# Layer 1's convolution norm: GpSimd adds the blocks and their squares ahead of one product of ones each, a gate tile later

## The chip, the cores and the metric

One core of a Trainium2 chip runs the whole kernel. The metric is the device time of one launch in microseconds (us), the median over several launches. The engines are named TensorE (PE; its weight loads are shown apart, PEld), VectorE (DVE), ScalarE (ACT), GpSimd (POOL) and SyncE (SP), which issues the weight transfers.

## The reference

A backbone of two layers. Each layer projects its normed input once, feeds three parallel branches (attention, a Conformer convolution, a short gated convolution), merges them by sigmoid gates, and adds a SwiGLU feed-forward. Layer 0 works on 256 latent and 256 context tokens, layer 1's branches on the 256 latent tokens alone. The change is in the layer norm of the convolution branch, over its 256 channels:

```python
def layer_norm(x, g, b):
    mu = jnp.mean(xf, axis=-1, keepdims=True)
    var = jnp.mean(jnp.square(xf - mu), axis=-1, keepdims=True)
    y = (xf - mu) * lax.rsqrt(var + EPS)
    return (y * g.astype(jnp.float32) + b.astype(jnp.float32)).astype(x.dtype)

def conformer_conv(glu_in, dw, dw_b, ln_g, ln_b, w_out):
    a, g = jnp.split(glu_in, 2, axis=-1)
    u = depthwise_conv(a * jax.nn.sigmoid(g), dw) + dw_b
    u = jax.nn.silu(layer_norm(u, ln_g, ln_b))
    return u @ w_out

def merge_branches(gate_in, y_att, y_conv, y_sc, w_o):
    g_att, g_conv, g_sc = jnp.split(jax.nn.sigmoid(gate_in), N_BRANCH, axis=-1)
    return (g_att * y_att + g_conv * y_conv + g_sc * y_sc) @ w_o
```

## The kernel before

Channels lie on the 128 partitions, tokens along the free axis, so the 256 convolution channels are two blocks, `ACC[:, 0]` and `ACC[:, 1]`. Each engine runs its own program in a fixed, hand-written order, and the engines meet at semaphores.

**Products.** Every float32 weight is split into a high and a low part so that TensorE can multiply with three fast products (lines 2000 to 2002). A weight piece arrives in one of four slots `Wraw` by a transfer that SyncE issues as soon as the slot's last residual is out (`load`, line 448, waits on `lo_done`). ScalarE converts it to `Whi` (line 399, `split_hi`, first waiting until the slot's last tile is done), VectorE makes the residual `Wlo` (line 410, `split_lo`), and TensorE's `chunk()` waits for that. Both helpers are called `look` and run three pieces ahead of TensorE (`AHEAD = 3`). GpSimd's `look` only counts.

**The branch stage** of a layer is eight groups. In a group TensorE makes two gate tiles (24 products each, from wide pieces 128x1024) and two output tiles (6 products each, from narrow pieces 128x256): groups 0 to 3 the outputs of the short convolution, groups 4 to 7 those of the Conformer convolution. A product has 512 columns in layer 0 and 256 in layer 1. ScalarE's `group` copies each gate tile out by a tanh into `TG` (line 783) once the output of the group before that used the same half of `TG` is drained. VectorE's `group` joins tanh and output (lines 1743 and 1748), which frees the output's bank. Tiles go round four PSUM banks.

**The norm** is woven into groups 2 and 3. VectorE finishes `ACC` (line 1780, semaphore `conv_a`). TensorE multiplies it with a matrix of ones, which gives the mean over channels in a bank; VectorE centres `ACC` (`centred`, line 1760), ScalarE squares it into `SQ` (`mean_squares`, line 1063, `conv_sq`), TensorE multiplies the squares with ones, ScalarE takes the root (`root`, line 801), and VectorE's `scaled` takes the reciprocal (line 1360) and applies it, gain and bias (lines 1768 and 1771). Then ScalarE's tanh, VectorE's product (line 1788, `conv_s`) and ScalarE's and VectorE's high and low part (lines 830 and 1367) make the operand `CO0` that the output tiles of group 4 wait for (`op_lo`). Root and tanh lie in different tables of ScalarE, which shows as ACT_TABLE_LOAD.

In layer 0 GpSimd adds the two blocks of `ACC`, and later the two of `SQ`, into `SUM`, and TensorE does one product of ones each (`of_sum`, line 2604), the mean after gate tile 1 of group 2 and the squares after gate tile 0 of group 3. In layer 1 TensorE does two products for each (`over_channels`, line 2564), the mean after gate tile 0 of group 2 and the squares between groups 2 and 3. In layer 1 alone eight transposes ahead of the mean (`gate_row`, line 2317) make a row that ScalarE copies into `LINES`.

Of the kernel before, what the change touches and what calls it, by code (L numbers as in the profile page):

```python
# [12 lines left out]
CH = 256  # L13
# [30 lines left out]
BEFORE_LAYER = 3  # L44
ROOT_AFTER = 12
LAST_BRANCH, LAST_FF = 39, 67
MEAN_AFTER = [1, 0]
PARTS = 4
PART = DT // PARTS

# [115 lines left out]
def build(nc, x, c, ctx_in, c_ctx, w_mod, b_mod, ln1_g, w_in, q_a_norm_g, w_q_b, kv_a_norm_g,  # L166
# [6 lines left out]
    with stack:  # L173
# [463 lines left out]
        def _(pool):  # L637
# [55 lines left out]
            for l in range(DEPTH):  # L693
                TQ = NS[l] * SEQ
                nxt = ahead(projection_kinds(l), HEAD_KINDS)

                def step_in():
                    look(next(nxt))

                clear_sum(stat_root(l, 0))  # L700
                if l == 0:
                    next(nxt)
                for _ in range(5 if l else 4):
                    step_in()
                at.square.n += 2
                for _ in range(2):
                    add_square(TQ)
                    step_in()
                at.square.next()
                for _ in range(9):  # L710
                    step_in()
                pool.wait_ge(tap_head, l + 1)
                pool.wait_ge(root_done, stat_root(l, 2))
                for w in range(TAPS_BEFORE, TAPS):
                    pool.wait_ge(pool_step, step.now())
                    v = mark(pool.tensor_scalar(by_stream(SUM[:, :], l), U[:, 1, 0:NS[l], w:w + SEQ],  # L716
                                                PAR[:, l, CDW + 2 * w + 1:CDW + 2 * w + 2], None, ALU.mult))
                    pool.wait_ge(pool_step, v)
                    ins = pool.tensor_tensor(by_stream(ACC[:, 1, :], l), by_stream(ACC[:, 1, :], l),  # L719
                                             by_stream(SUM[:, :], l), ALU.add)  # L720
                    if w < TAPS - 1:
                        mark(ins)
                    else:
                        ins.then_inc(tap_tail, 1)
                pool.wait_ge(tap_tail, l + 1)
                for kind in ["plain", "keys", queries_kind(1)]:
                    look(kind)
                with at.loop(pool, PAIRS - 2, chunks=4):
                    for kind in pair_looks(0):
                        look(kind)  # L730
                for p in range(PAIRS - 2, PAIRS):
                    for kind in pair_looks(p):
                        look(kind)
                for kind in ahead(["plain"] * 4, branch_kinds(l)):
                    look(kind)
                with at.loop(pool, 3, chunks=8):
                    for kind in ahead(branch_kinds(l), branch_kinds(l)):
                        look(kind)
                for kind in ahead(branch_kinds(l), ["plain"] * AHEAD):
                    look(kind)  # L740
                if l == 0:
                    pool.wait_ge(root_done, stat_root(l, 2))
                    pool.wait_ge(conv_a, 1)
                    pool.tensor_tensor(SUM[:, :], ACC[:, 0, :], ACC[:, 1, :], ALU.add).then_inc(conv_summed, 1)
                    pool.wait_ge(conv_sq, 1)
                    pool.tensor_tensor(SUM[:, :], SQ[:, 0, :], SQ[:, 1, :], ALU.add).then_inc(conv_summed, 1)
                clear_sum(stat_root(l, 3))
                for j in range(WHOLE if l == 0 else DT - 1):
                    look()
                    add_square(TQ)  # L750
                if l == 0:
                    add_halves()
                else:
                    look()
                    at.square.next()
                for g, n in enumerate(FF_GROUPS if l == 0 else []):
                    last = g == len(FF_GROUPS) - 1
                    with at.loop(pool, n // 2, chunks=4):
                        for _ in range(4):
                            look()  # L760
                    if last:
                        clear_sum(stat_root(l, 4))
                        for j in range(WHOLE):
                            look()
                            add_square(TQ)
                        add_halves()
                    else:
                        with at.loop(pool, 2, chunks=4):
                            for _ in range(4):
                                look()  # L770

        @block.scalar
        def _(act):
# [101 lines left out]
            for l in range(DEPTH):  # L875
# [162 lines left out]
                def group(mean=None, squares=None, inside=None):  # L1038

                    before = outs[-2:]  # L1040
                    for j in range(2):
                        look(next(nxt))
                        if before:
                            act.wait_ge(drained[before[j].bank], before[j].drained)
                        copy_out(TG[:, j, 0:TQ], TQ, ACT.Tanh, 0.5)
                        if j == MEAN_AFTER[l] and mean:
                            mean()
                        if j == 0 and squares:
                            squares()
                    for j in range(2):  # L1050
                        if j and inside:
                            inside()
                        look(next(nxt))
                        outs.append(at.tile())
# [21 lines left out]
                group()  # L1076
                group()
                group(mean=mean_squares)
                if l:
                    root(TQ, CH, stat_root(l, 3))  # L1080
                    group()
                else:
                    group(squares=lambda: root(TQ, CH, stat_root(l, 3)))
                normalised()
                def merged_out(i):

# [171 lines left out]
        def _(dve):  # L1258
# [233 lines left out]
            for l in range(DEPTH):  # L1492
# [227 lines left out]
                def group(i, taps=0, mean=None, squares=None, inside=None):  # L1720

                    gates, before = [], outs[-2:]
                    if squares and l:
                        of_squares = at.tile()
                    for j in range(2):
                        look_and_fold(next(nxt))
                        gates.append(at.tile())
                        if j == 0 and squares and not l:
                            of_squares = at.tile()
                        if j == MEAN_AFTER[l] and mean:  # L1730
                            mean()
                        if j == MEAN_AFTER[l] and squares:
                            squares(of_squares)
                        do_taps(max(0, min(2, taps - 2 * j)))
                    for j in range(2):
# [237 lines left out]
        def _(pe):  # L1973
# [401 lines left out]
            for l in range(DEPTH):  # L2375
# [182 lines left out]
                            if j == 3:  # L2558
                                last.then_inc(tile_done, 1)

                def over_channels(src):
                    t = new_tile()
                    for j in range(2):
                        last = pe.matmul(banks[t.bank][:, 0:TQ], ONES[:, :], src[:, j, 0:TQ], start=j == 0, stop=j == 1)
                    last.then_inc(tile_done, 1)

                mla(at.operand.n)
                for _ in range(3):
                    mla()
# [1 line left out]
                def group(o0, mean=None, squares=None, gates_done=None):  # L2571

                    for j in range(2):
                        tile_of(P, DT, H, 0, TQ)
                        if j == MEAN_AFTER[l] and mean:
                            mean()
                        if j == 0 and squares:
                            squares()
                    if gates_done:
                        gates_done()  # L2580
                    pe.wait_ge(op_lo, at.operand.n)
                    for j in range(2):
                        tile_of(P, 2, O, o0, TQ)

                def mean_over_channels():
                    if l:
                        gate_row()
                        pe.wait_ge(conv_a, l + 1)
                        over_channels(ACC)
                    else:  # L2590
                        pe.wait_ge(conv_summed, 1)
                        of_sum()

                def squares_over_channels():
                    if l:
                        pe.wait_ge(conv_sq, l + 1)
                        over_channels(SQ)
                    else:
                        pe.wait_ge(conv_summed, 2)
                        of_sum()  # L2600

                def of_sum():
                    t = new_tile()
# [3 lines left out]
                group(SO0)  # L2607
                group(SO0)
                group(SO0, mean=mean_over_channels)
                if l:  # L2610
                    squares_over_channels()
                    group(SO0)
                else:
                    group(SO0, squares=squares_over_channels)
                at.operand.n += 2
                for g in range(4, 8):
                    group(CO0, gates_done=sum_branch if l == 0 and g == BRANCH_FOLDS[-1] // 4 + 1 else None)
# [116 lines left out]
```

## Time and profile before

| | us |
|---|---|
| median of 3 runs (lowest, highest) | 1228.86 (1228.07, 1229.69) |
| the profiled execution's own time | 1228.0 |
| its span, first to last instruction | 1226.2 |
| TensorE busy | 1205.7 (98%) |
| VectorE busy | 851.7 (69%) |
| ScalarE busy | 516.5 (42%) |
| GpSimd busy | 189.1 (15%) |

The granted clock is 0.999 of full speed over the span. All times in the rows below are us from the span's start. A timeline line gives the start, the time taken, engine, line, operation, out<-in, shapes and how many instructions it merges; in brackets how long the engine idled ahead of it and who ended that. Matmuls overlap, so their starts tell the pace, not their durations. Layer 1's groups 2, 3 and 4 begin on TensorE at about 955.7, 965.6 and 973.0 us.

### The profile page before, as it was taken

Reading aid. Unit: us, or ns where it says so; the run is one execution under the profiler, and the core shown is the slowest. Engines: PE = TensorE matmul, PEld = TensorE weight load, DVE = VectorE, ACT = ScalarE, POOL = GpSimd, SP = SyncE. Lnnn points to the kernel's source line nnn. Section 1 sums busy time; section 2 is a strip of 40 time slices with the busy share of each in tenths; the row PEclk is TensorE's granted clock in tenths of the full one; section 3 lists DMA queues with packets and bytes.
Section 4 is the critical chain, followed back from the end, with each engine's and each line's share of the span. In section 5 each row is a group of like instructions: output and inputs, shape, how many; then the busy total and the mean of one; then the engine's idle time right before and its main releaser. Section 6 shows DMA issues by size and latency. Waiting matters only on the chain.

```text
span 1226.2 us, 18387 instructions
## 1 busy us (share of the span) xinstructions
PE 1205.7 (98%) x7170; PEld 1017.3 (83%) x7170; DVE 851.7 (69%) x1245; ACT 516.5 (42%) x850; POOL 189.1 (15%) x158
## 2 busy tenths in 40 slices
PE   7999999999999999999999999999999999999997
PEld 5677777788888898888888888889789998999996
DVE  4665866586887487678765655799887777655555
ACT  4342555522433352222222223465664555544443
POOL 0005994000001200000000000302970002000000
PEclk9999999999999999999999999999999999999999
DMA  9947322134464536457655664335444674766662
GB/s 291 318 143 215 83 54 69 35 87 123 117 174 130 160 102 193 152 163 215 190 188 158 212 191 147 104 86 151 119 127 114 157 206 142 219 188 184 183 186 86
DMA packets 265254, 188.91 MB, mean 154 GB/s; under 512 B 16035, under 2 KB 250833, under 8 KB 265169
## 3 DMA queue, kind: packets, MB, share of 16 engines
q1 hardware_dynamic: 264832, 187.60, 52.4%
q8 instruction: 57, 0.93, 0.3%
q14 instruction: 28, 0.23, 0.1%
q10 hardware_dynamic: 337, 0.15, 0.0%
HBM read 186.67 MB, written 1.05 MB: 153 GB/s over the span
## 4 chain that ended last, share of the span: by engine, by line
PE 89%; DVE 4%; ACT 3%; SPq 2%; issue 2%; DMA 1%; DVEq 0%; ACTq 0%
PE bank L2000 21%; PE bank L2001 20%; PE bank L2002 20%; PE scores L2476 3%; PE bank L2456 2%; PE bank L2458 2%; PE bank L2457 2%; PE probsT L2485 2%; PE attended L2499 1%; ACT Whi L399 1%; SPq L491 1%; DVE Wlo L410 1%; PE bank L2555 1%; PE bank L2556 1%; PE bank L2557 1%
## 5 line engine op out<-in xcount | busy, mean ns | idle before, releaser
L410 DVE TENSOR_TENSOR Wlo<-Wraw,Whi 128x1024 fp32r<-128x1024 f32 (+3 forms) x294 | 323.2, 1105 | 116.1 <-ACT Whi L399 115.0
L2000 PE MATMUL bank<-Hhi,Whi 128*128 128x512 f32 (+1 forms) x1114 | 378.5, 340 | 1.3 <-DVE Wlo L410 1.1
L2001 PE MATMUL bank<-Hlo,Whi 128*128 128x512 f32 (+1 forms) x1114 | 374.5, 336 | 0.0
L2002 PE MATMUL bank<-Hhi,Wlo 128*128 128x512 f32 (+1 forms) x1114 | 374.4, 336 | 0.0
L399 ACT ACTIVATE Whi<-Wraw 128x1024 fp32r<-128x1024 f32 (+1 forms) x296 | 270.8, 928 | 132.1 <-PE bank L2002 71.7
L2000 PEld LDWEIGHTS bank<-Hhi,Whi 128*128 128x128 f32 x1114 | 211.3, 190 | 31.0 <-issue 6.4
L2001 PEld LDWEIGHTS bank<-Hlo,Whi 128*128 128x128 f32 x1114 | 211.4, 190 | 22.5 <-issue 1.0
L2002 PEld LDWEIGHTS bank<-Hhi,Wlo 128*128 128x128 f32 x1114 | 211.4, 190 | 22.0
L2000 PE MATMUL bank<-Uhi,Whi 128*128 128x512 f32 (+1 forms) x350 | 128.4, 367 | 0.2 <-issue 0.2
L2002 PE MATMUL bank<-Uhi,Wlo 128*128 128x512 f32 (+1 forms) x350 | 126.5, 362 | 0.0
L2001 PE MATMUL bank<-Ulo,Whi 128*128 128x512 f32 (+1 forms) x350 | 126.5, 361 | 0.0
L667 POOL TENSOR_TENSOR SUM<-SUM,V 128x512 f32<-128x512 f32 (+1 forms) x23 | 31.0, 1347 | 534.2 <-ACT V L793 534.0
L716 POOL TENSOR_SCALAR SUM<-U,PAR 128x512 f32<-128x512 f32 (+1 forms) x56 | 81.2, 1449 | 63.6 <-DVE ACC L1561 58.3
L2000 PEld LDWEIGHTS bank<-Uhi,Whi 128*128 128x128 f32 x350 | 66.0, 189 | 11.7 <-issue 2.0
L2002 PEld LDWEIGHTS bank<-Uhi,Wlo 128*128 128x128 f32 x350 | 66.0, 189 | 10.3
L2001 PEld LDWEIGHTS bank<-Ulo,Whi 128*128 128x128 f32 x350 | 66.1, 189 | 9.9 <-issue 0.2
L1808 DVE SCALAR_TENSOR_TENSOR X<-bank,MOD,X 128x256 f32<-128x256 f32 x64 | 28.1, 478 | 55.3 <-PE bank L2002 52.8
L719 POOL TENSOR_TENSOR ACC<-ACC,SUM 128x512 f32<-128x512 f32 (+1 forms) x56 | 64.6, 1153 | 4.7
L1310 DVE SCALAR_TENSOR_TENSOR G<-ATT,CV,G 128x1024 f32<-128x1024 f32 x50 | 64.8, 1320 | 0.0
L783 ACT ACTIVATE V<-bank 128x512 f32<-128x512 f32 (+1 forms) x48 | 24.4, 508 | 95.3 <-PE bank L2002 95.2
L1848 DVE SCALAR_TENSOR_TENSOR Z<-V,bank 128x512 f32<-128x512 f32 (+1 forms) x44 | 24.4, 553 | 41.9 <-PE bank L2002 23.5
L1220 ACT ACTIVATE Uhi<-PR 128x512 fp32r<-128x512 f32 x22 | 13.9, 632 | 91.4 <-DVE PR L1855 91.4
(292 smaller groups left out, 1766.4 us busy)
## 6 DMA issues: line engine op xcount, KB each, us to landing
Wraw<-in_w_ff SPq DMA_DIRECT2D x126, 512.0 KB, 3.9
Wraw<-in_w_in SPq DMA_DIRECT2D x78, 512.0 KB, 4.0
ATT<-in_w_mod SPq DMA_DIRECT2D x58, 512.0 KB, 4.5
Wraw<-in_w_o SPq DMA_DIRECT2D x16, 512.0 KB, 4.3
ACC<-in_w_mod SPq DMA_DIRECT2D x14, 512.0 KB, 4.5
Wraw<-in_w_mla_o SPq DMA_DIRECT2D x8, 512.0 KB, 3.5
ATT<-in_w_mod SPq DMA_DIRECT2D x12, 256.0 KB, 7.6
Wraw<-in_w_kv_b SPq DMA_DIRECT2D x12, 256.0 KB, 3.7
```

Source lines behind the costliest of these rows:

```text
L399: last = act.activation(hi, raw, ACT.Copy)
L410: last = eng.tensor_tensor(lo, raw, hi.bitcast(F32), ALU.subtract)
L667: pool.tensor_tensor(SUM[:, 0:n], SUM[:, 0:n], SQ[:, slot, 0:n], ALU.add).then_inc(sq_summed, 1)
L716: v = mark(pool.tensor_scalar(by_stream(SUM[:, :], l), U[:, 1, 0:NS[l], w:w + SEQ], PAR[:, l, CDW + 2 * w + 1:CDW + 2 * w + 2], None, ALU. ...
L719: ins = pool.tensor_tensor(by_stream(ACC[:, 1, :], l), by_stream(ACC[:, 1, :], l), by_stream(SUM[:, :], l), ALU.add)
L1310: last = dve.scalar_tensor_tensor(acc(s), raw, c, acc(s), mult, add)
L1808: last = dve.scalar_tensor_tensor(X[:, m, half[s]], banks[t.bank][:, half[s]], MOD[:, l, m + mod * DT, s:s + 1], X[:, m, half[s]], mult, add)
L2000: pe.matmul(dst, sh, mh, start=j == 0, stop=False)
L2001: pe.matmul(dst, sh, ml, start=False, stop=False)
L2002: last = pe.matmul(dst, sl, mh, start=False, stop=j == k - 1)
L2456: pe.matmul(dst, Whi[:, slot, w], Hhi[:, j, 0:TQ], start=j == 0, stop=False)
L2476: pe.matmul(S[h][:, 0:kt * P], Qb[0:NOPE + ROPE, h, col:col + P], Kb[0:NOPE + ROPE, h, k0 * P:(k0 + kt) * P], start=True, stop=True).then_ ...
```

## The change

In layer 1 the norm takes layer 0's form. GpSimd adds the blocks of `ACC` and of `SQ` (the first TQ columns), TensorE does one product with ones for each, the mean's (with the gate row ahead of it) after gate tile 1 of group 2 instead of gate tile 0, the squares' after gate tile 0 of group 3 instead of ahead of it. ScalarE squares after its second tanh of group 2 and takes the root after its first tanh of group 3; VectorE centres after the second look of group 2 and scales after the second look of group 3 instead of the first. `over_channels` goes.

```diff
-MEAN_AFTER = [1, 0]
+MEAN_AFTER = 1
 # gpsimd
-                if l == 0:
-                    pool.wait_ge(root_done, stat_root(l, 2))
-                    pool.wait_ge(conv_a, 1)
-                    pool.tensor_tensor(SUM[:, :], ACC[:, 0, :], ACC[:, 1, :], ALU.add).then_inc(conv_summed, 1)
-                    pool.wait_ge(conv_sq, 1)
-                    pool.tensor_tensor(SUM[:, :], SQ[:, 0, :], SQ[:, 1, :], ALU.add).then_inc(conv_summed, 1)
+                pool.wait_ge(root_done, stat_root(l, 2))
+                pool.wait_ge(conv_a, l + 1)
+                pool.tensor_tensor(SUM[:, 0:TQ], ACC[:, 0, 0:TQ], ACC[:, 1, 0:TQ], ALU.add).then_inc(conv_summed, 1)
+                pool.wait_ge(conv_sq, l + 1)
+                pool.tensor_tensor(SUM[:, 0:TQ], SQ[:, 0, 0:TQ], SQ[:, 1, 0:TQ], ALU.add).then_inc(conv_summed, 1)
                 clear_sum(stat_root(l, 3))
 # scalar
-                        if j == MEAN_AFTER[l] and mean:
+                        if j == MEAN_AFTER and mean:
                             mean()
-                if l:
-                    root(TQ, CH, stat_root(l, 3))
-                    group()
-                else:
-                    group(squares=lambda: root(TQ, CH, stat_root(l, 3)))
+                group(squares=lambda: root(TQ, CH, stat_root(l, 3)))
 # vector
-                    if squares and l:
-                        of_squares = at.tile()
                     for j in range(2):
                         look_and_fold(next(nxt))
                         gates.append(at.tile())
-                        if j == 0 and squares and not l:
+                        if j == 0 and squares:
                             of_squares = at.tile()
-                        if j == MEAN_AFTER[l] and mean:
+                        if j == MEAN_AFTER and mean:
                             mean()
-                        if j == MEAN_AFTER[l] and squares:
+                        if j == MEAN_AFTER and squares:
                             squares(of_squares)
 # tensor
-                        if j == MEAN_AFTER[l] and mean:
+                        if j == MEAN_AFTER and mean:
                             mean()
                 def mean_over_channels():
                     if l:
                         gate_row()
-                        pe.wait_ge(conv_a, l + 1)
-                        over_channels(ACC)
-                    else:
-                        pe.wait_ge(conv_summed, 1)
-                        of_sum()
+                    pe.wait_ge(conv_summed, 2 * l + 1)
+                    of_sum()
 
                 def squares_over_channels():
-                    if l:
-                        pe.wait_ge(conv_sq, l + 1)
-                        over_channels(SQ)
-                    else:
-                        pe.wait_ge(conv_summed, 2)
-                        of_sum()
+                    pe.wait_ge(conv_summed, 2 * l + 2)
+                    of_sum()
...
-                if l:
-                    squares_over_channels()
-                    group(SO0)
-                else:
-                    group(SO0, squares=squares_over_channels)
+                group(SO0, squares=squares_over_channels)
```

## Rows read from the trace of the kernel before

**Rows 1.** The page, part 1: busy us (share of the span) xinstructions.

```profile
PE 1205.7 (98%) x7170; PEld 1017.3 (83%) x7170; DVE 851.7 (69%) x1245; ACT 516.5 (42%) x850; POOL 189.1 (15%) x158
```

**Rows 2.** Waits of PEld, 905 to 1030: engine line waited for, us, times, longest.

```profile
PEld bank L2000 <- DVE Wlo L410: 0.3, 1, 0.3
```

**Rows 3.** Timeline of PE and PEld around the mean in layer 1.

```profile
958.57 1.03 PE L2317 MATMUL bank<-IDN,MOD 128*128 128x128 f32 x8
...
959.60 0.73 PEld L2564 LDWEIGHTS bank<-ACC,ONES 128*128 128x128 f32 x4 [0.24 <-DVE ACC L1780]
...
960.68 0.28 PE L2001 MATMUL bank<-Hlo,Whi 128*128 128x256 f32 x1
960.80 0.28 PE L2002 MATMUL bank<-Hhi,Wlo 128*128 128x256 f32 x1
```

**Rows 4.** Timeline of PE around the squares in layer 1.

```profile
964.87 1.02 PE L2564 MATMUL bank<-V,ONES 128*128 128x256 f32 x4
...
965.85 0.28 PE L2001 MATMUL bank<-Hlo,Whi 128*128 128x256 f32 x1
```

**Rows 5.** GpSimd's adds: layer 0's timeline, VectorE beside it, and layer 1's taps (min/median/max ns).

```profile
310.71 1.30 POOL L746 TENSOR_TENSOR SUM<-V 128x512 f32<-128x512 f32 x1 [7.31 <-ACT V L1063]
...
311.62 1.48 DVE L410 TENSOR_TENSOR Wlo<-Wraw,Whi 128x1024 fp32r<-128x1024 f32 x1 [2.17 <-ACT Whi L399]
...
L719 POOL TENSOR_TENSOR ACC<-ACC,SUM x28: 723/788/1777, 853.5 to 913.5; 128x256 f32<-128x256 f32 x28
```

**Rows 6.** Timeline of DVE in layer 1, groups 2 to 4.

```profile
960.77 0.76 DVE L1760 SCALAR_TENSOR_TENSOR ACC<-bank,ACC 128x256 f32<-128x256 f32 x2 [0.89 <-PE bank L2564]
963.26 1.23 DVE L410 TENSOR_TENSOR Wlo<-Wraw,Whi 128x1024 fp32r<-128x1024 f32 x1 [1.74 <-ACT Whi L399]
965.05 1.23 DVE L410 TENSOR_TENSOR Wlo<-Wraw,Whi 128x1024 fp32r<-128x1024 f32 x1 [0.57 <-ACT Whi L399]
966.20 0.41 DVE L1743 SCALAR_TENSOR_TENSOR Z<-V,bank 128x256 f32<-128x256 f32 x1
966.64 0.42 DVE L1748 TENSOR_TENSOR G<-G,Z 128x256 f32<-128x256 f32 x1
...
968.45 1.75 DVE L1360 RECIPROCAL RSTD<-ROOT 128x256 f32<-128x256 f32 x1
...
971.68 1.22 DVE L410 TENSOR_TENSOR Wlo<-Wraw,Whi 128x1024 fp32r<-128x1024 f32 x1
973.10 1.23 DVE L410 TENSOR_TENSOR Wlo<-Wraw,Whi 128x1024 fp32r<-128x1024 f32 x1 [0.20 <-ACT Whi L399]
...
977.40 0.76 DVE L1367 SCALAR_TENSOR_TENSOR Ulo<-ACC,Uhi 128x256 fp32r<-128x256 f32 x2 [0.48 <-ACT Uhi L830]
...
979.23 1.23 DVE L410 TENSOR_TENSOR Wlo<-Wraw,Whi 128x1024 fp32r<-128x1024 f32 x1 [0.74 <-ACT Whi L399]
```

**Rows 7.** Timeline of ACT in layer 1, groups 2 and 3.

```profile
961.56 0.72 ACT L1063 ACTIVATE V<-ACC 128x256 f32<-128x256 f32 x2 [1.27 <-DVE ACC L1760]
962.19 1.04 ACT L399 ACTIVATE Whi<-Wraw 128x1024 fp32r<-128x1024 f32 x1
...
965.98 1.28 ACT L801 ACT_TABLE_LOAD   x1 [0.65 <-PE bank L2564]
967.27 0.39 ACT L801 ACTIVATE ROOT<-bank 128x256 f32<-128x256 f32 x1
967.55 0.41 ACT L399 ACTIVATE Whi<-Wraw 128x256 fp32r<-128x256 f32 x1
```

**Rows 8.** Timeline of PE at the end of group 4 and the start of group 5.

```profile
980.13 0.28 PE L2002 MATMUL bank<-Uhi,Wlo 128*128 128x256 f32 x1
980.51 0.39 PE L2000 MATMUL bank<-Hhi,Whi 128*128 128x256 f32 x1
```

**Rows 9.** Waits of PEld in layer 0's groups 2 to 4, 300 to 340.

```profile
PEld bank L2000 <- issue: 0.5, 2, 0.2
```

**Rows 10.** Issues of line 448, 971 to 979: DMA to landing, us min/median/max.

```profile
DMA to landing us min/median/max: 2.3/4.5/5.7
```

More of the change, by code:

```diff
@@ L2559, in mla @@
                                 last.then_inc(tile_done, 1)
[L2561 to L2565, printed above, removed]
                 mla(at.operand.n)
```

## The prediction

> **What bounds the kernel now.** The page comes first. TensorE is busy 98% of the span [rows 1], so time is gained only by taking work or waits from TensorE, and lost wherever another engine hands something to it too late. The waits of its weight loads over layer 1's branch stage come next: beside a wait of 0.24 us for the convolution's result [rows 3] there is one for a weight residual, 0.3 us in all of 125 us [rows 2]. Then TensorE's own timeline, which gives what the changed products cost, and last VectorE's and ScalarE's timelines over the same 20 us, which show how far these two run ahead of it. I write A3, B3 for the two wide weight pieces (128x1024) of group 3, c3, d3 for its two narrow ones, and likewise for other groups. In a group TensorE issues gate tile 0, gate tile 1, output 0, output 1. A gate tile is 24 products, an output 6, one each 0.12 us (starts 960.68 and 960.80 [rows 3]): 2.88 and 0.72 us, a group 7.2 us. Each look of VectorE is one piece: d of the same group first, then A, B and c of the next.
>
> **The change on TensorE.** Removed are one of two products for the mean and one of two for the squares. The mean's pair starts at 959.60; the first product behind it has a start distorted by the switch, the second has 960.68, and in an even stream it is 0.12 after the first: 960.68 - 0.12 - 959.60 = 0.96 us [rows 3]. The squares' pair costs 965.85 - 0.12 - 964.87 = 0.86 us [rows 4]. It is four records, so one product of 256 columns is 0.43. Saved: 0.53 and 0.43. The 0.24 us wait on `conv_a` [rows 3] goes too: VectorE has the result at 959.60 at the latest, when that wait ends; GpSimd's adds of 256 columns take 0.8 us, the median of 28, and 1.8 at the most [rows 5], so SUM is there at 960.5, at the latest at 961.5, and TensorE, which now issues gate tile 1 (2.88) ahead of the gate row, wants it at 958.57 + 2.88 + 0.79 = 962.24. (The gate row's eight transposes: 0.79, from 958.57 to the wait's start at 959.36.) On TensorE alone the change is worth 0.53 + 0.43 + 0.24 = 1.20 us. Nothing else there changes in number; the two added GpSimd instructions queue in front of nothing but its clearing of SUM, which waits for the root anyway.
>
> **The change on the other engines.** The mean and the squares each come a gate tile later on TensorE, and all that follows on ScalarE and VectorE does too. The question is whether it still lies beside other work. I put the new times down by the hand-overs of the old.
> 1. Mean product at 962.24. Old: product 959.60, VectorE's centring 960.77, so 1.17 with four records; with two, 0.43 less: 962.98, rounded down to 962.95 [rows 3, 6].
> 2. ScalarE squares 0.79 after the centring began (960.77, 961.56), converts B3 0.63 later (962.19) and VectorE takes its residual 1.07 after that (962.19, 963.26) [rows 6, 7]: 963.74, 964.37, 965.44. Before, A3's conversion stood here; it now goes ahead of the mean. GpSimd's add of the squares, 964.4 to 965.2, is ready 1.8 us ahead of its product (966.99).
> 3. VectorE has merged output 0 of group 2, and freed its bank and the tanh tile, 2.01 us after that look began (965.05 to 966.64 + 0.42) [rows 6]: 967.45. TensorE reaches gate tile 1 of group 3, which needs that bank, at 962.24 + 0.43 + 1.44 + 2.88 + 0.43 = 967.42. No wait to speak of.
> 4. ScalarE's tanh of gate tile 0 needs it as well: 967.48. The root comes after the tanh now, with its table load: 0.4 for the tanh, then 1.30 to the root (965.98 to 967.27), 0.28 to the next conversion [rows 7]: A4 at 969.45. VectorE: 970.52, done 971.75. TensorE wants A4 at 967.42 + 2.88 + 1.44 = 971.74: a tie.
> 5. Now VectorE does the scaling, one look later than before. 1.15 from the wide look (as 965.05 to 966.20), then 3.23 us for reciprocal, two products, two scalings (968.45 to 971.68) [rows 6]: it starts at 971.67 and lets the look at B4 begin at 974.90. In the old order the 3.23 us lay ahead of A4, and B4 began at 973.10 [rows 6]. **The shift is +1.80 us.**
> 6. TensorE wants B4 for gate tile 1 of group 4 at 971.74 + 2.88 = 974.62 and gets it at 974.90 + 1.23 = 976.13: a new wait of 1.5 us. Outputs 0 and 1 of group 4 need the convolution operand, whose low part ended at 977.40 + 0.76 = 978.16 [rows 6] and now ends 1.80 later, 979.96; TensorE is there at 976.2 + 2.88 = 979.1: a second wait of 0.9 us.
> 7. Behind that, ScalarE converts A5 only when the operand is out, since it stands in a wait for VectorE until then. Before, A5's residual began at 979.23 and ended at 980.46 [rows 6], and TensorE began group 5 at 980.51 behind a wait on it [rows 8]. From B4 to A5 VectorE and ScalarE hand over to each other without slack, so A5 ends at 982.26 and TensorE starts group 5 at 982.31.
>
> So the 1.20 us of TensorE and the wait of 0.26 us ahead of 980.51 are spent: before and after, the start of group 5 hangs on the same chain through VectorE and ScalarE, and that chain is 1.80 us later. From group 5 on the order is as before; the residual at 980.51 is the one TensorE waits for in the whole stage [rows 2], so nothing gives the 1.80 back, and transfers are cleared by the same looks, shifted alike. Layer 0 has this order already, and there TensorE waits for no residual [rows 9]; but its products have 512 columns, while a wide look and a table load don't grow with them, so its example does not carry over.
>
> Sum: the profiled execution took 1228.0 us (span 1226.2), so 1229.8; the median of the runs is 0.86 above it: 1228.86 + 1.80 = **1230.7 us**.
>
> **A rule weighed.** In layer 0 a wide look beside GpSimd's add of the squares lasted 1.48 us [rows 5] instead of 1.23 [rows 6]. The Trainium skill (SBUF — State Buffer, "Who interferes with whom") says that a VectorE instruction with two SBUF inputs and a GpSimd instruction that reads SBUF exclude each other for a whole instruction. By it, the look at B3 would start only when the add ended: the sum stays 1.80 with an add of 0.8 us and would be 2.60 with one of 1.8. The trace shows a delay of 0.25 us, not the 0.39 of overlap that was left (310.71 + 1.30 - 311.62).
>
> **The rivals.**
> *TensorE's saving comes through.* If scaling or the root come out quicker than in steps 4 and 5, so that B4 is ready by 974.62, 1.20 us are saved, and with the wait ahead of 980.51 (980.51 - 980.13 - 0.12 = 0.26 [rows 8]) 1.46: 1227.4. For it: 1.2 us less work on the bounding engine. Against it: steps 2 to 5 are fixed hand-overs, and B4 would have to be 1.5 us earlier. Chance 0.13.
> *GpSimd's squares get in the chain's way.* The add lies at 964.4 to 965.2 and the look at B3 starts at 965.44; a slower add (up to 1.8 us [rows 5]) meets it. Price from nothing to 0.8 (964.4 + 1.8 - 965.44), taken as 0.25, as in layer 0 [rows 5], and every later step moves with it: +2.05, 1230.9. At the full 0.8 it is 1231.5. Chance 0.12.
> *Slower by over 0.2%: the transfer of B5.* It starts when B4's residual is done, 976.13 + 0.2, 1.8 us later than before. ScalarE needs it landed to leave 1.05 + 1.23 us for conversion and residual before TensorE wants B5 at 982.31 + 2.88 = 985.19; the point from which it decides is a landing 6.5 us after issue. Before, transfers issued in this stretch took 2.3 to 5.7 us [rows 10]. With 8 us TensorE would wait 1.5 more: +3.3, 1232.2. Chance 0.15.
> *As forecast,* a chance of 0.60. Its own range: twelve hand-overs, each read to 0.05 or 0.1 us, and the root's and the bank's ties can add up to 0.7 us either way: 1230.0 to 1231.4, and a median itself moves by about 0.8 (their spread), so 1229.2 to 1232.2.
>
> **How the numbers follow.** 0.2% is 2.5 us, about what a measurement of this kernel can tell from no change: 1226.4 to 1231.3 counts as the same. The forecast lies 0.6 inside the upper edge. Of its 0.60, 0.16 lies above it; the contention rival gives 0.04, the transfer 0.13: slower 0.33. The TensorE rival lies inside the bound, and only its lower tail and the runs' spread beyond it: faster 0.05. Same 0.62. The range runs from 1227.2, just under the TensorE rival, to 1233.0, past the transfer rival's 1232.2 by the runs' spread.
>
> **What would show it.** Right: half as many records on the product of ones in layer 1, no wait for the shifted convolution there; a TensorE wait for a weight residual of some 1.5 us at about 974.6, one of 0.9 us for Ulo at about 979, one of about 0.8 us at 981.5; the start of group 5 at 982.3 instead of 980.5; VectorE's reciprocal at 971.7 instead of 968.45. Wrong: the reciprocal ahead of 970.2 (then B4 is in time and the kernel gains), the start of group 5 less than 1 us from 980.5, or a wait on a transfer in group 5. It is also wrong if layer 0 or the feed-forward stage differ by more than some tenths: there the instructions are the same.

## The result and the profile after

The changed kernel takes 1229.66 us (median of 22 runs, 1228.59 to 1231.37), the kernel before, on the same chips, 1227.99 us (22 runs, 1226.68 to 1229.69): a ratio of 1.0014, 95% interval 1.0009 to 1.0020, or 1.7 us more. The profiled execution of the changed kernel took 1229.27 us with a span of 1227.5.

The spans differ by 1.3 us. I split them at two points on TensorE, the first product of group 2 and the first of group 5, and call the time between them D. All positions of the prediction can be read against the start of group 2, which lies at 955.69 before and at 955.12 after.

| stretch, us | before | after | difference |
|---|---|---|---|
| start to group 2 | 955.69 | 955.12 | -0.57 |
| group 2 to group 5 (D) | 24.82 | 26.64 | +1.82 |
| group 5 to the end | 245.69 | 245.74 | +0.05 |

The first difference is no effect of the change: over the ten profiles of this document, whose programs are alike up to there, group 2 starts anywhere from 954.69 to 955.85. The page after, part 1, differs from [rows 1] by the four TensorE records and the two GpSimd instructions:

```profile
PE 1205.2 (98%) x7166; PEld 1016.4 (83%) x7166; DVE 851.6 (69%) x1245; ACT 516.5 (42%) x850; POOL 190.5 (16%) x160
```

The waits of TensorE's weight loads over the same stretch as [rows 2], 905 to 1030, after the change (line 1993 is the 2000 of before, 1362 the 1367). The 0.3 us for a residual has become 2.2, and a wait for the operand's low part is new:

```profile
PEld bank L1993 <- DVE Wlo L410: 2.2, 2, 1.4
...
PEld bank L1993 <- DVE Ulo L1362: 0.9, 1, 0.9
```

TensorE's timeline after the change, for [rows 3, 4, 8]. A single product of ones costs 962.30 - 0.12 - 961.75 = 0.43 us at the mean, 967.24 - 0.12 - 966.49 = 0.63 at the squares; then the three waits, at 974.18, 978.49 and 980.89:

```profile
960.88 1.03 PE L2310 MATMUL bank<-IDN,MOD 128*128 128x128 f32 x8
961.75 0.60 PE L2584 MATMUL bank<-SUM,ONES 128*128 128x256 f32 x2
...
962.30 0.28 PE L1994 MATMUL bank<-Ulo,Whi 128*128 128x256 f32 x1
...
966.49 0.59 PE L2584 MATMUL bank<-SUM,ONES 128*128 128x256 f32 x2
...
967.24 0.28 PE L1994 MATMUL bank<-Hlo,Whi 128*128 128x256 f32 x1
...
974.18 0.28 PE L1995 MATMUL bank<-Hhi,Wlo 128*128 128x256 f32 x1
975.63 0.39 PE L1993 MATMUL bank<-Hhi,Whi 128*128 128x256 f32 x1 [1.18 <-DVE Wlo L410]
...
978.49 0.28 PE L1995 MATMUL bank<-Hhi,Wlo 128*128 128x256 f32 x1
979.47 0.39 PE L1993 MATMUL bank<-Uhi,Whi 128*128 128x256 f32 x1 [0.70 <-DVE Ulo L1362]
...
980.89 0.28 PE L1995 MATMUL bank<-Uhi,Wlo 128*128 128x256 f32 x1
981.76 0.39 PE L1993 MATMUL bank<-Hhi,Whi 128*128 128x256 f32 x1 [0.60 <-DVE Wlo L410]
```

Counted from one start to the next, less the 0.12 of a product, the waits are 1.33, 0.86 and 0.75 us. VectorE's timeline after the change, for [rows 6], shows what TensorE waited for: the look at A4 at 969.99, the scaling behind it, and B4's look only at 974.36:

```profile
962.38 0.76 DVE L1753 SCALAR_TENSOR_TENSOR ACC<-bank,ACC 128x256 f32<-128x256 f32 x2 [1.40 <-PE bank L2584]
964.88 1.22 DVE L410 TENSOR_TENSOR Wlo<-Wraw,Whi 128x1024 fp32r<-128x1024 f32 x1 [1.74 <-ACT Whi L399]
...
969.99 1.23 DVE L410 TENSOR_TENSOR Wlo<-Wraw,Whi 128x1024 fp32r<-128x1024 f32 x1 [1.63 <-ACT Whi L399]
971.13 1.75 DVE L1355 RECIPROCAL RSTD<-ROOT 128x256 f32<-128x256 f32 x1
...
974.36 1.22 DVE L410 TENSOR_TENSOR Wlo<-Wraw,Whi 128x1024 fp32r<-128x1024 f32 x1
...
978.65 0.76 DVE L1362 SCALAR_TENSOR_TENSOR Ulo<-ACC,Uhi 128x256 fp32r<-128x256 f32 x2 [0.48 <-ACT Uhi L829]
...
980.48 2.45 DVE L410 TENSOR_TENSOR Wlo<-Wraw,Whi 128x1024 fp32r<-128x1024 f32 x2 [0.73 <-ACT Whi L399]
```

And ScalarE's, for [rows 7]: the tanh of gate tile 0 waits for VectorE, the table load stands behind it, and A4's conversion (968.91) behind the root:

```profile
966.93 0.38 ACT L782 ACTIVATE V<-bank 128x256 f32<-128x256 f32 x1 [1.47 <-DVE G L1741]
967.33 1.28 ACT L800 ACT_TABLE_LOAD   x1
968.63 0.39 ACT L800 ACTIVATE ROOT<-bank 128x256 f32<-128x256 f32 x1
968.91 1.05 ACT L399 ACTIVATE Whi<-Wraw 128x1024 fp32r<-128x1024 f32 x1
```

### The profile page after: what moved, and what is told of

It is laid out like the page before. It is cut to its first block, busy times and chain, and to the rows that moved or that the text cites. A ratio compares the mean times of both kernels' runs of the same rounds, so it can differ in the third digit from the quotient of the medians.

```text
span 1227.5 us, 18382 instructions
## 1 busy us (share of the span) xinstructions
PE 1205.2 (98%) x7166; PEld 1016.4 (83%) x7166; DVE 851.6 (69%) x1245; ACT 516.5 (42%) x850; POOL 190.5 (16%) x160
## 3 DMA queue, kind: packets, MB, share of 16 engines
HBM read 186.67 MB, written 1.05 MB: 153 GB/s over the span
## 4 chain that ended last, share of the span: by engine, by line
PE 87%; DVE 4%; ACT 3%; issue 2%; ACTq 0%; DVEq 0%
PE bank L1993 20%; PE bank L1994 20%; PE bank L1995 20%; PE scores L2469 3%; PE bank L2449 2%; PE bank L2451 2%; PE bank L2450 2%; PE probsT L2478 2%; PE attended L2492 1%; ACT Whi L399 1%; DVE Wlo L410 1%; PE bank L2548 1%; PE bank L2549 1%; PE bank L2550 1%; PE bank L2102 1%
```

## The experiments

The theory: the start of group 5 on TensorE is set by a chain through VectorE and ScalarE, which the new places of mean and squares make 1.8 us later. The rivals: GpSimd's adds cost the time, by being late or by getting in VectorE's way; or TensorE's new order does, through banks. All edits are in layer 1 alone. Measured ratios are to the kernel before, run beside each. D is read from one profile of each kernel; the kernel that was profiled twice gave 27.31 and 27.32. In the code below `...` marks lines left out.

| kernel | D, us | against before | ratio (95% interval) |
|---|---|---|---|
| before | 24.82 | | |
| the change | 26.64 | +1.82 | 1.0014 (1.0009 to 1.0020) |
| place alone, pairs of products | 27.34 | +2.52 | 1.0020 (1.0010 to 1.0029) |
| adds alone, old places | 25.04 | +0.22 | 0.9998 (0.9989 to 1.0007) |
| change, root behind the look at A4 | 25.61 | +0.79 | 1.0005 (0.9996 to 1.0014) |
| the same, d4 and A5 ahead of the operand | 24.85 | +0.03 | 0.9999 (0.9990 to 1.0008) |
| change, scaling ahead of the look at A4 | 27.31 | +2.49 | 1.0013 (1.0004 to 1.0022) |
| the same again | 27.32 | +2.50 | 1.0009 (1.0000 to 1.0018) |
| change, squares added twice | 27.15 | +2.33 | 1.0014 (1.0005 to 1.0023) |
| before, squares summed, looks early | 24.01 | -0.81 | 0.9987 (0.9978 to 0.9996) |

**The place alone.** The changed kernel with `over_channels` back and no adds on GpSimd.

```diff
...
                     if l:
                         gate_row()
-                    pe.wait_ge(conv_summed, 2 * l + 1)
-                    of_sum()
+                        pe.wait_ge(conv_a, l + 1)
+                        over_channels(ACC)
...
-                    pe.wait_ge(conv_summed, 2 * l + 2)
-                    of_sum()
+                    if l:
+                        pe.wait_ge(conv_sq, l + 1)
+                        over_channels(SQ)
...
```

GpSimd's adds stand under `if l == 0` again, as before the change.

> The place alone: in layer 1 mean and squares at the changed kernel's places, but made by pairs of products as before, with no adds on GpSimd. Theory (the place makes the chain late, the single products shorten it a little): the centring starts 0.54 us later after its product's start (1.17 instead of 0.63), all behind it too, D is 27.2, 0.5 to 0.6 more than with the change and 2.4 more than before. Rival (GpSimd's adds cost the time): D back to 24.8 to 25.3.

D is 27.34 and the time 1.0020, or 2.5 us more than before: near the theory's 27.2, and nothing like the rival's 25. Without any add of GpSimd in layer 1 the kernel is slower still. Of VectorE's timeline in this kernel (group 2 starts at 955.28) two lines say it: the centring lies 7.70 us and B4's look 19.94 us behind that start, against 7.26 and 19.24 with the change. The mean's second product gives 0.44 of the 0.70; the other 0.26 come at the squares, where ScalarE's table load now waits 0.28 us for the pair and with the change waits for nothing.

```profile
962.98 0.76 DVE L1754 SCALAR_TENSOR_TENSOR ACC<-bank,ACC 128x256 f32<-128x256 f32 x2 [1.97 <-PE bank L2558]
...
975.22 1.22 DVE L410 TENSOR_TENSOR Wlo<-Wraw,Whi 128x1024 fp32r<-128x1024 f32 x1
```

**The adds alone.** The kernel before with GpSimd's adds and single products in layer 1, at the old places.

```diff
...
                     if l:
                         gate_row()
-                        pe.wait_ge(conv_a, l + 1)
-                        over_channels(ACC)
+                    pe.wait_ge(conv_summed, 2 * l + 1)
+                    of_sum()
...
```

The squares' product is changed likewise, and GpSimd's two adds are those of the change.

> The adds alone: in layer 1 GpSimd adds and TensorE makes single products, but at the places of the kernel before (mean after gate tile 0 of group 2, squares ahead of group 3). Measure: D, 24.82 us before, 26.64 with the change. Theory (the place is what costs): TensorE waits for GpSimd's add of the blocks, 0.9 us on top of the 0.24 it waited for the convolution, the mean is 0.4 us later, the squares' single product gives 0.43 back, B4's look is 0.2 to 0.4 us later than before, and D is 25.1, at most 25.3. Rival (the adds on GpSimd cost the time by themselves): D near 26.6, as with the change.

D is 25.04, as the theory had it. What the adds cost is one wait, here in TensorE's weight loads; it is 0.91 us longer than the 0.24 of [rows 3]:

```profile
959.51 0.30 PEld L2596 LDWEIGHTS bank<-SUM,ONES 128*128 128x128 f32 x2 [1.15 <-POOL SUM L743]
```

On TensorE the two single products give that back (0.53 and 0.43 us). D grows by 0.22 all the same, because the chain through VectorE is later: the centring by 0.48 us (5.56 behind the start of group 2 instead of 5.08) and A5's look, the last that group 5 waits for, still by 0.19 (23.73 instead of 23.54).

Together the two runs split the change: moving both sums by a gate tile costs 2.5 us, and single products at the new place, where GpSimd's latency is hidden, take 0.7 of that back (27.34 - 26.64). No run moves one of the two sums alone.

**The root behind the look.** The changed kernel with ScalarE's root after its conversion of A4.

```diff
                     for j in range(2):
                         look(next(nxt))
+                        if j and l and squares:
+                            squares()
                         if before:
                             act.wait_ge(drained[before[j].bank], before[j].drained)
                         copy_out(TG[:, j, 0:TQ], TQ, ACT.Tanh, 0.5)
...
-                        if j == 0 and squares:
+                        if j == 0 and squares and not l:
                             squares()
```

> The changed kernel with one thing moved: in layer 1 ScalarE converts A4 ahead of the root with its table load instead of behind it. Theory: the conversion of A4 starts at once behind the tanh, 1.7 us earlier, its residual too, so VectorE's reciprocal starts 1.15 us earlier, when the root is out, B4's look and all behind it 1.15 us earlier, D 25.5; the wait for B4 falls from 1.33 to some 0.3 us, the one for the operand stays near 0.9. Rival (TensorE's new places or GpSimd cost the time): D stays at 26.6.

D falls by 1.03 us to 25.61, where 25.5 was expected. Not a product nor an add has moved on TensorE or GpSimd, so neither rival can claim this: one swap in ScalarE's order takes more than half of the loss back. The wait for B4 fell from 1.33 to 0.29, the one for the operand stayed.

**And A5 early.** Beside that, ScalarE converts d4 and A5 ahead of its wait for the operand.

```diff
...
                     last.then_inc(conv_t, 1)
-                    act.wait_ge(conv_s, l + 1)
-                    for j in range(2):
-                        operand(Uhi[:, CO0 + j, 0:TQ], ACC[:, j, 0:TQ], z=False, scale=0.5)
+                    if l == 0:
+                        conv_operand()
...
                         look(next(nxt))
...
+                        if j and between:
+                            between()
...
```

> As the one before, and in layer 1 ScalarE converts d4 and A5 ahead of its wait for the convolution operand instead of behind it. Theory: A5's residual follows the operand's low part on VectorE without a wait, at 1.3 us after its start instead of 1.83, TensorE's wait of 0.75 us ahead of group 5 goes, D is 24.8, that of before, and the time is that of before within 0.1%. Rival (the start of group 5 hangs on a transfer or on VectorE alone): D as in the one before, 25.5.

D is 24.85 and the time that of before, as expected. The whole loss is undone by ScalarE's order alone, with the change's own order on TensorE, GpSimd and VectorE untouched. TensorE still waits 0.86 us for the operand and 0.30 for B4; that is where the saved products have gone.

**The scaling ahead of A4**, twice.

```diff
-                        if j == MEAN_AFTER and squares:
+                        if j == (0 if l else MEAN_AFTER) and squares:
                             squares(of_squares)
```

> The changed kernel with one thing moved: in layer 1 VectorE scales ahead of its look at A4 instead of behind it. Measure: D, from the first product of group 2 to the first of group 5 on TensorE, 24.82 us before and 26.64 with the change. Theory (the chain VectorE-ScalarE from the centring to A5 sets the start of group 5, and the look at A4 ahead of the scaling is part of why it is late): the reciprocal starts when the root is out, about 2.1 us earlier, A4's residual about 2.3 us later, so TensorE waits 2.2 us for A4, B4's look starts 0.9 us earlier, and D is 25.7: 0.9 less than with the change, 0.9 more than before. Rival (the adds on GpSimd, or TensorE's new places themselves, cost the time): D stays at 26.6.

Here the expectation missed: D is 27.31, not 25.7. The chain did what was said: the reciprocal started 2.0 us earlier (14.02 us behind the start of group 2 instead of 16.01), and A5's residual was done 0.9 us earlier against the start of group 2 (25.74 us behind it, 26.59 with the change). But TensorE came later than that. Its timeline, around the wait for A4 and 1.4 us further on:

```profile
971.01 0.28 PE L1995 MATMUL bank<-Uhi,Wlo 128*128 128x256 f32 x1
973.35 0.39 PE L1993 MATMUL bank<-Hhi,Whi 128*128 128x256 f32 x1 [2.06 <-DVE Wlo L410]
...
974.76 0.32 PE L1995 MATMUL bank<-Hhi,Wlo 128*128 128x256 f32 x1
974.88 0.41 PE L1993 MATMUL bank<-Hhi,Whi 128*128 128x256 f32 x1
975.10 0.41 PE L1994 MATMUL bank<-Hlo,Whi 128*128 128x256 f32 x1
975.31 0.41 PE L1995 MATMUL bank<-Hhi,Wlo 128*128 128x256 f32 x1
```

The products' pace goes from 0.12 to 0.21 us. The table of stretches (us, then busy time and instructions of PE, PEld, DVE, ACT and POOL, the granted clock, DMA share, GB/s) has a granted clock of 0.50 there, the lower of its two levels, 1.2 for 2.4 GHz:

```profile
973.40:974.90 1.50, 1.50 (x13) 1.50 (x14) 1.47 (x3) 0.07 (x1) 0.00 (x0) 0.99 0.21 17
974.90:978.20 3.30, 3.30 (x18) 3.30 (x17) 2.78 (x9) 1.15 (x4) 0.00 (x0) 0.50 1.03 282
978.20:980.20 2.00, 2.00 (x18) 2.00 (x18) 1.27 (x3) 1.10 (x2) 0.00 (x0) 0.98 0.55 147
```

Half a clock over 3.3 us costs some 1.6 us, and 25.7 + 1.6 is the 27.3 measured. To see whether that was chance, the kernel ran once more:

> The kernel with the scaling ahead of the look at A4 once more. In its first profile TensorE waited 2.06 us for A4, and from 1.7 us after that wait its products came every 0.21 us instead of 0.12 for some 3.4 us, with a granted clock of 0.61 over those 4 us; D was 27.31. If the fall follows the wait of 2 us, it is there again at the same place and D is 27.3. If it was a chance of that execution, the products stay at 0.12 us and D is 25.7, as first expected.

It was there again, right behind the wait, with D at 27.32:

```profile
973.98 0.39 PE L1993 MATMUL bank<-Hhi,Whi 128*128 128x256 f32 x1 [2.06 <-DVE Wlo L410]
974.20 0.36 PE L1994 MATMUL bank<-Hlo,Whi 128*128 128x256 f32 x1
974.37 0.41 PE L1995 MATMUL bank<-Hhi,Wlo 128*128 128x256 f32 x1
974.58 0.41 PE L1993 MATMUL bank<-Hhi,Whi 128*128 128x256 f32 x1
```

Both profiles have it. Of the unprofiled runs the time and the granted clock over the whole span are on record. The 7 of the 21 runs of this kernel whose clock was 0.998 or 0.999 took 1228.41 us in the mean, 0.84 more than the 39 runs at the same clock among the 66 of before that ran beside the experiments: the 0.9 first expected, without a fall. The other 14, both profiled ones among them, took 1229.92. So the fall seems to be absent from about a third of the executions, as far as a clock averaged over the whole span can tell. In these profiles it follows a wait of 2.2 us in one piece, where three waits of 1.33, 0.86 and 0.75 us with work between them had none.

But a wait doesn't decide it alone. At about 1031 us, behind the branch stage, TensorE waits 1.8 us for an operand of ScalarE in all ten profiles. Eight keep a clock of 1.00 behind it. Two, that of the kernel with A5 early and that of the last kernel below, fall to 0.50 for some 3.4 us, and their stretch from group 5 to the end is 1 us longer (246.7 us instead of 245.7). First the kernel with A5 early, its wait and the stretch behind it, then the same stretch of the one with the place alone:

```profile
PE bank L2044 <- ACT Hhi L837: 1.8, 1, 1.8
...
1030.00:1035.00 5.00, 3.86 (x21) 3.89 (x22) 4.40 (x11) 2.43 (x5) 0.00 (x0) 0.70 0.14 41
...
1030.00:1035.00 5.00, 3.17 (x28) 2.97 (x27) 4.03 (x7) 1.79 (x4) 0.00 (x0) 1.00 0.39 114
```

So behind the same wait the fall comes in some executions and not in others. This one lies outside D but in the times: the 27 runs of before with a clock under 0.998 took 1.2 us more than those 39. What decides it stays open.

**The squares added twice.** The changed kernel; GpSimd's second add lies over VectorE's look at B3.

```diff
                 pool.wait_ge(conv_sq, l + 1)
+                if l:
+                    v = mark(pool.tensor_tensor(SUM[:, 0:TQ], SQ[:, 0, 0:TQ], SQ[:, 1, 0:TQ], ALU.add))
+                    pool.wait_ge(pool_step, v)
                 pool.tensor_tensor(SUM[:, 0:TQ], SQ[:, 0, 0:TQ], SQ[:, 1, 0:TQ], ALU.add).then_inc(conv_summed, 1)
```

> The changed kernel, with GpSimd adding the two blocks of squares twice over (the same sum). The second add lies over VectorE's look at B3, which starts some 0.9 us after the first add. By layer 0's row, where such a look lasted 1.48 us beside an add, the look lasts 0.25 us longer and all behind it comes 0.25 us later: D 26.9. By full exclusion (the Trainium skill, SBUF - State Buffer, Who interferes with whom) the look would end some 0.7 us later, and D would be 27.3. The product of the squares still finds its sum ready. If GpSimd's adds had nothing to do with it at all, D stays at 26.64.

GpSimd's and VectorE's timelines in this kernel:

```profile
964.49 0.74 POOL L748 TENSOR_TENSOR SUM<-V 128x256 f32<-128x256 f32 x1
...
964.57 1.73 DVE L410 TENSOR_TENSOR Wlo<-Wraw,Whi 128x1024 fp32r<-128x1024 f32 x1 [1.74 <-ACT Whi L399]
```

The look lasted 1.73 us instead of 1.22, 0.51 more, and D grew by the same 0.51 to 27.15, between the 26.9 and the 27.3 of the two readings: this look is on the chain. The two overlapped for 964.49 + 0.74 - 964.57 = 0.66 us. In layer 0 it was 0.25 more for 0.39 of overlap [rows 5]. The changed kernel has a third case, the add of `ACC`'s blocks beside A3's look:

```profile
959.12 0.79 POOL L743 TENSOR_TENSOR SUM<-ACC 128x256 f32<-128x256 f32 x1 [45.46 <-DVE ACC L1773]
...
959.62 1.36 DVE L410 TENSOR_TENSOR Wlo<-Wraw,Whi 128x1024 fp32r<-128x1024 f32 x1 [0.32 <-ACT Whi L399]
```

That look lasted 1.36 us, against 1.23 in the kernel with the place alone, which has no such add: 0.13 more for 0.29 of overlap. All three times it is the overlap less about 0.15. That is nearer to the Trainium skill's rule (SBUF — State Buffer, "Who interferes with whom"), by which the two contend for a shared pair of ports that is an exclusive lock, than my reading of a fixed 0.25 us; where the 0.15 lie isn't shown. In the changed kernel neither add cost D anything: behind A3's look VectorE idles 1.40 us for the mean's product, and the add of the squares ended at 964.72, 0.16 us ahead of B3's look. Ratio and D part here (1.0014 against 2.33 us, 0.19%); the interval covers both.

**The squares summed, and looks early.** The kernel before, with four things in layer 1: GpSimd sums the squares for one product at the old place, while the mean stays a pair; ScalarE converts A4 ahead of its tanh of gate tile 0, and d4 and A5 ahead of the operand; VectorE takes A4's residual between reciprocal and scaling.

```diff
 # gpsimd
+                else:
+                    pool.wait_ge(root_done, stat_root(l, 2))
+                    pool.wait_ge(conv_sq, l + 1)
+                    pool.tensor_tensor(SUM[:, 0:TQ], SQ[:, 0, 0:TQ], SQ[:, 1, 0:TQ], ALU.add).then_inc(conv_summed, 1)
...
 # scalar, group 3
+                        if early and j == 0:
+                            t = at.tile()
+                            look(next(nxt))
+                            act.wait_ge(drained[before[j].bank], before[j].drained)
+                            act.activation(TG[:, j, 0:TQ], banks[t.bank][:, 0:TQ], ACT.Tanh, scale=0.5).then_inc(drained[t.bank], 1)
+                            continue
...
 # scalar, group 4
+                        if j and between:
+                            between()
...
 # vector
                             squares(of_squares)
+                        if l and j and squares:
+                            applied()
...
 # tensor
-                    if l:
-                        pe.wait_ge(conv_sq, l + 1)
-                        over_channels(SQ)
-                    else:
-                        pe.wait_ge(conv_summed, 2)
-                        of_sum()
+                    pe.wait_ge(conv_summed, 3 if l else 2)
+                    of_sum()
...
```

> A version built on the kernel before, in layer 1 alone: the mean as before (a pair of products after gate tile 0 of group 2); GpSimd adds the squares and TensorE makes one product of them, at the old place; ScalarE converts A4 ahead of its first tanh of group 3, and d4 and A5 ahead of its wait for the convolution operand; VectorE takes the residual of A4 between reciprocal and scaling. Theory (the start of group 5 is the later of TensorE's own work and the chain): TensorE saves 0.43 us of product, A4 is ready 1.1 us ahead, B4 1.2 us ahead of when it is wanted, the operand's low part ends 0.2 us earlier than before and 0.3 us ahead of output 0, A5 0.2 us ahead of group 5: no waits, D is 24.0, 0.8 less than before, and the time is 0.07% under that of before. Rival (another wait is next, the operand or a transfer): D 24.4 to 24.8.

D is 24.01, and the time 1226.42 against 1227.89 us. The ratio's interval, 0.9978 to 0.9996, lies below 1 and holds the 0.9993 that 0.81 us of D stand for. So this kernel is faster than the one before, and with it than the change. The medians lie 1.47 us apart, more than D accounts for; where the rest lies isn't shown, nor which of the four things are needed, since they ran together. TensorE runs from group 2 to group 5 without a wait for a residual or the operand; its timeline at the start of group 5, where [rows 8] have one of 0.26 us:

```profile
978.73 0.28 PE L2027 MATMUL bank<-Uhi,Wlo 128*128 128x256 f32 x1
978.85 0.28 PE L2025 MATMUL bank<-Hhi,Whi 128*128 128x256 f32 x1
```

## Why the prediction was right

The forecast was 1228.86 + 1.80 = 1230.7 us. Measured against the kernel before on the same chips the change cost 1.67 us, and the profile puts +1.82 where the forecast had +1.80. The 1.0 us between 1230.7 and 1229.66 is nearly all the starting point: the three runs that were shown had a median 0.87 above that of all 22.

Step by step, in us behind the start of group 2 (forecast less 955.69, measured less 955.12):

| step | forecast | measured |
|---|---|---|
| mean's product (1) | 6.55 | 6.63 |
| centring (1) | 7.26 | 7.26 |
| residual of B3 (2) | 9.75 | 9.76 |
| output 0's bank free (3) | 11.76 | 11.77 |
| residual of A4 (4) | 14.83 | 14.87 |
| reciprocal (5) | 15.98 | 16.01 |
| residual of B4 (5) | 19.21 | 19.24 |
| operand's low part done (6) | 24.27 | 24.29 |
| group 5 on TensorE (7) | 26.62 | 26.64 |

The first two rows hold a little luck. The mean's product came 0.08 us later than forecast, because the gate row ahead of it took 0.87 us and not 0.79, and VectorE's centring followed it by 0.63 us and not 0.71. The two errors cancel, and everything behind hangs on the second row.

TensorE's own saving was right too, but for step 3's "no wait to speak of": the bank is free at 11.77 and wanted at about 11.8, and the squares' product cost 0.63 us instead of 0.43. With the adds at the old places it cost 0.42, so the hand-over of the bank is the likely cause, though no run shows it by itself. It costs nothing, since TensorE waits later anyway. The waits were 1.33, 0.86 and 0.75 us for 1.5, 0.9 and 0.8.

The shape of the argument is what the runs bear out: the place costs (place alone, +2.52), the adds hardly do (adds alone, +0.22), and the loss goes away when two ScalarE orders change (+0.79, then +0.03). Nothing gives the 1.8 us back behind group 5 (+0.05). The rivals: TensorE's saving didn't come through, and GpSimd's add cleared the look by 0.16 us, though the doubled add shows that what it adds to the look goes into D in full. The transfer of B5 was never waited for: in the profile after, ScalarE converts B5 straight behind its tanh, at 980.62, with no wait on a transfer.

Where a step failed it was in an expectation, not in the forecast: a wait was priced at its own length, and a wait of 2.2 us in one piece brought 1.6 us more by the clock. The forecast has the same gap: it prices every wait at its own length and doesn't weigh the clock at all. The change's three waits left it at 1.00 in the profile; with one wait of 2.2 us instead, it could have missed by as much.

## What to carry to other kernels

Work taken off the busiest engine is worth something only if what it feeds, and what feeds it back, is no later: write down the hand-overs of the other engines' in-order queues one by one, from rows, until they meet the busy engine again. A schedule that is free at one tile size need not be at half of it. Here the same order had no wait for a residual in layer 0 and three waits in layer 1; the table load (1.28 us) and the conversion and residual of a wide piece (1.05 and 1.23 us) last the same in both, while a product has half the columns. That this is the reason is argued from these rows; no run changed the tile size. And before moving products between engines, look at the order of an idle engine's queue: an instruction that stands behind a wait it doesn't need (A4 behind the root, A5 behind the operand) was worth 1.79 us here (26.64 - 24.85), the single products 0.7.

## What the runs showed of the hardware

- TensorE's granted clock fell to 0.50 behind a single wait of 2.2 us, for some 3.3 us, in both profiles of one kernel, 1.5 and 0.3 us after the wait's end; behind waits of 1.33, 0.86 and 0.75 us it stayed at 1.00. Behind a wait of 1.8 us at about 1031 us it fell in two of ten profiles, so the same wait can go either way.
- A VectorE subtraction with two SBUF inputs beside a GpSimd add took 0.51 us longer for 0.66 us of overlap, 0.25 for 0.39 and 0.13 for 0.29.
- Swapping ScalarE's table cost the load alone: from the root's load to the root 968.63 - 967.33 = 1.30 us, with the tanh ending at 967.31.
- A float32 product with ones of 256 columns cost TensorE 0.43 us (0.42 at the old place of the squares), as much as 3.6 of the split weights' products of the same size, 0.12 us each.
